# A filter's first layer on GpSimd: products of three inputs in one instruction of 384 columns

## The reference, cut to what matters

```
z = concat([t[:, None], cos(ang), -sin(ang)], axis=-1)     # 256 positions x 33 inputs
h = sin(fr * (z @ w1 + b1))                                # 33 -> 64 hidden
h = sin(fr * (h @ w2 + b2))
h = sin(fr * (h @ w3 + b3))
h = h @ w4                                                 # then decay, convolution by FFT
```

## Time and profile before

| | us |
|---|---|
| median of 3 runs | 2062.11 |
| the profiled execution's own time | 2062.2 |
| its span | 2060.3 |
| TensorE busy (9213 matmuls) | 2010.0 |
| VectorE busy | 1322.0 |
| ScalarE busy | 924.0 |
| GpSimd busy | 384.6 |

### The profile page before, as it was taken

The page is one execution under the profiler, slowest core; times in us unless marked ns, Lnnn a source line. Parts: engine busy times, 40 slices in busy tenths (PEclk is TensorE's granted clock), DMA queues, the critical chain, the costliest instruction groups (busy, mean ns, idle before and its releaser), DMA issues.

```text
span 2060.3 us, 23555 instructions
## 1 busy us (share of the span) xinstructions
PE 2010.0 (98%) x9213; PEld 1595.5 (77%) x9213; DVE 1322.0 (64%) x1684; ACT 924.0 (45%) x1218; POOL 384.6 (19%) x588
## 2 busy tenths in 40 slices
PE   5899999999999999999999999999999999999999
PEld 1268788777878878787888888888888888878887
DVE  4867678798675779878875665644555445444443
ACT  1155534555644544354554444544444444433332
POOL 0000004999999950000000000000000000000000
PEclk9999999999999999999999999999999999999999
DMA  9977667555576675554446555555556655655654
GB/s 344 367 244 252 207 221 243 170 175 167 175 227 190 190 227 183 161 176 148 153 145 204 184 184 185 183 191 191 190 185 193 195 184 188 200 164 187 201 185 162
DMA packets 206242, 407.93 MB, mean 198 GB/s; under 512 B 8826, under 2 KB 15027, under 8 KB 205491
## 3 DMA queue, kind: packets, MB, share of 16 engines
q1 hardware_dynamic: 190480, 376.07, 55.6%
q10 hardware_dynamic: 13892, 23.88, 3.5%
q0 software_dynamic: 1760, 6.49, 1.6%
HBM read 404.31 MB, written 2.10 MB: 197 GB/s over the span
## 4 chain that ended last, share of the span: by engine, by line
PE 72%; POOL 19%; DVE 4%; DMA 3%; issue 2%; ACTq 0%; ACT 0%; SPq 0%; DVEq 0%; POOLq 0%
PE ps L432 44%; PE ps L439 22%; POOL proj L2316 17%; PE pm L520 4%; DMA raw<-in_ada_w 2%; POOL h3T L2316 1%; DVE mod_part L1161 1%; DVE raw_lo L410 1%; PE pm L532 1%; POOL proj L2295 1%; PE ps L520 1%; PE pm L895 0%; PE pm L584 0%; DMA proj<-in_z 0%; DMA rows_b<-in_hgrn_norm_g 0%
## 5 line engine op out<-in xcount | busy, mean ns | idle before, releaser
L410 DVE TENSOR_TENSOR raw_lo<-raw,w_hi 128x1024 fp32r<-128x1024 f32 (+1 forms) x648 | 800.1, 1238 | 565.5 <-ACT w_hi L401 555.8
L401 ACT ACTIVATE w_hi<-raw 128x1024 fp32r<-128x1024 f32 (+1 forms) x648 | 680.3, 1051 | 788.4 <-PE ps L439 761.4
L432 PE MATMUL ps<-w_hi,h_hi 128*128 128x512 f32 (+1 forms) x2336 | 934.6, 401 | 3.7 <-DVE h_lo L977 3.0
L432 PE MATMUL ps<-w_hi,h_lo 128*128 128x512 f32 (+1 forms) x2336 | 908.6, 389 | 0.0
L439 PE MATMUL ps<-raw_lo,h_hi 128*128 128x512 f32 (+1 forms) x2336 | 622.8, 388 | 7.7 <-DVE raw_lo L410 7.6
L432 PEld LDWEIGHTS ps<-w_hi,h_hi 128*128 128x128 f32 x2336 | 441.4, 189 | 103.4 <-issue 9.6
L439 PEld LDWEIGHTS ps<-raw_lo,h_hi 128*128 128x128 f32 x2336 | 436.8, 189 | 102.6 <-DVE raw_lo L410 12.2
L432 PEld LDWEIGHTS ps<-w_hi,h_lo 128*128 128x128 f32 x2336 | 441.6, 189 | 92.9 <-issue 7.4
L2316 POOL TENSOR_TENSOR proj<-proj 128x128 f32<-128x128 f32 x264 | 178.9, 683 | 12.9
L2316 POOL TENSOR_TENSOR proj<-proj,w1T 128x128 f32<-128x128 f32 x165 | 101.8, 625 | 12.3 <-DMA proj<-in_z 5.1
L432 PE MATMUL ps<-w_hi,hid_hi 128*128 128x512 f32 x256 | 100.8, 394 | 0.0
(11 more groups left out here) (322 smaller groups left out, 1146.2 us busy)
## 6 DMA issues: line engine op xcount, KB each, us to landing
raw<-in_w_in SPq DMA_DIRECT2D x136, 1024.0 KB, 5.3
raw<-in_w_ffn_gate SPq DMA_DIRECT2D x44, 1024.0 KB, 5.2
raw<-in_w_ffn_up SPq DMA_DIRECT2D x44, 1024.0 KB, 5.1
raw<-in_w_ffn_down SPq DMA_DIRECT2D x44, 1024.0 KB, 5.1
raw<-in_ada_w SPq DMA_DIRECT2D x32, 1024.0 KB, 7.5
raw<-in_w_out SPq DMA_DIRECT2D x32, 1024.0 KB, 5.2
proj<-in_ada_w ACTq DMA_DIRECT2D x16, 1024.0 KB, 5.2
raw<-in_w_br_hyena SPq DMA_DIRECT2D x8, 1024.0 KB, 5.2
```

The costliest lines, as they stand in the source:

```text
L401: nc.scalar.activation(w_hi[:, p % HRING, :, 0:gm.width(j)], raw[:, k % RING, e:e + HT, 0:gm.width(j)], ACT.Copy).then_inc(hi_done, 1)
L410: nc.vector.tensor_tensor(raw_lo[:, k % RING, e:e + HT, 0:gm.width(j)], raw[:, k % RING, e:e + HT, 0:gm.width(j)], w_hi[:, p % HRING, :, 0 ...
L432: nc.tensor.matmul(ps[pair][:, t, 0:gm.width(j)], l[:, tok], hi[:, i, 0:gm.width(j)], start=(k == 0 and l is x_hi), stop=False)
```

## The change

The products and their errors are made for the three inputs of a group at once: `p_`, `e_` and `q_` become tiles of 3x128 columns, read from `z_k` in one piece, and the weights are broadcast along the 128 positions of each of the three. A group has 9 such instructions of 384 columns. The running sum stays an input at a time, 8 instructions of 128 columns each. It is in a stricter order: where the errors of sum and product were interleaved in 9 stages an input, there are now 7 stages for a group's products and 7 for each of its inputs, 28 a group. A group thus has 33 instructions instead of 51, and all have 363 instead of 561. The three wide tiles and the two narrow ones lie in both halves of `proj`.

```diff
-        f_tmp = proj[:, 0, R_F + 9 * P:R_F + 16 * P].rearrange("p (q n) -> p q n", q=7)
+        f_wide = [proj[:, t, R_F + c * P:R_F + (c + FK) * P].rearrange("p (k n) -> p k n", k=FK) for t, c in ((0, 9), (0, 12), (1, 11))]
+        f_tmp = [proj[:, t, R_F + c * P:R_F + c * P + P] for t, c in ((0, 15), (1, 9))]
...
                 pool.wait_ge(sig(f"z_in{e % 2}"), 32 * (e // 2 + 1))
-                p_, e_, s_, b_, d_, t_, q_ = (f_tmp[:, q] for q in range(7))
+                p_, e_, q_ = f_wide
+                s_, b_ = f_tmp
                 acc = h3T[:]
-                for j in range(FK):
-                    z_, zh, zl = (z_k[e % 2][:, q, j] for q in range(3))
-                    w_, wh, wl = (w1T[:, q, e * FK + j:e * FK + j + 1].to_broadcast([P, P]) for q in range(3))
-                    n = 17 * (FK * e + j)
-                    for stage in (((p_, z_, w_, ALU.mult), (e_, zh, wh, ALU.mult)),
-                                  ((e_, e_, p_, ALU.subtract), (s_, acc, p_, ALU.add), (q_, zl, wh, ALU.mult)),
-                                  ((e_, e_, q_, ALU.add), (b_, s_, acc, ALU.subtract)),
-                                  ((q_, zh, wl, ALU.mult), (d_, s_, b_, ALU.subtract), (t_, p_, b_, ALU.subtract)),
-                                  ((e_, e_, q_, ALU.add), (d_, acc, d_, ALU.subtract)),
-                                  ((q_, zl, wl, ALU.mult), (t_, t_, d_, ALU.add)),
-                                  ((e_, e_, q_, ALU.add),),
-                                  ((t_, t_, e_, ALU.add),),
-                                  ((acc, s_, t_, ALU.add),)):
-                        for o, x, y, op in stage:
-                            g.tensor_tensor(o, x, y, op).then_inc(sig("sum_step"), 1)
-                            n += 1
-                        pool.wait_ge(sig("sum_step"), n)
+                z_, zh, zl = (z_k[e % 2][:, q] for q in range(3))
+                w_, wh, wl = (w1T[:, q, e * FK:e * FK + FK].unsqueeze(2).to_broadcast([P, FK, P]) for q in range(3))
+                n = (9 + 8 * FK) * e
+                products = (((p_, z_, w_, ALU.mult), (e_, zh, wh, ALU.mult)),
+                            ((e_, e_, p_, ALU.subtract), (q_, zl, wh, ALU.mult)),
+                            ((e_, e_, q_, ALU.add),), ((q_, zh, wl, ALU.mult),),
+                            ((e_, e_, q_, ALU.add),), ((q_, zl, wl, ALU.mult),),
+                            ((e_, e_, q_, ALU.add),))
+                sums = [(((s_, acc, p_[:, j], ALU.add),), ((b_, s_, acc, ALU.subtract),),
+                         ((p_[:, j], p_[:, j], b_, ALU.subtract),), ((b_, s_, b_, ALU.subtract),),
+                         ((b_, acc, b_, ALU.subtract), (p_[:, j], p_[:, j], e_[:, j], ALU.add)),
+                         ((p_[:, j], p_[:, j], b_, ALU.add),), ((acc, s_, p_[:, j], ALU.add),)) for j in range(FK)]
+                for stage in itertools.chain(products, *sums):
+                    for o, x, y, op in stage:
+                        g.tensor_tensor(o, x, y, op).then_inc(sig("sum_step"), 1)
+                        n += 1
+                    pool.wait_ge(sig("sum_step"), n)
                 pool.sem_inc(sig("z_used"), 1)
```

More of the change, by code:

```diff
@@ L1 @@
+import itertools
 import math
```

## The result

The changed kernel took 2080.65 us in the median of 6 runs (2072.48 to 2087.72), the kernel before 2060.97 us in the median of its 6 runs (2059.35 to 2063.93). The ratio is 1.0091, 95% interval 1.006 to 1.0123: 0.9% slower. It was forecast at 2074.3 us, between 2060 and 2086 us. Run again on another occasion the same kernel gave 2086.6 us in the median of 4 and 1.0113 (1.0085 to 1.0141). The profiled execution is a long one of the first six, 2086.15 us with a span of 2084.3 us, 24.0 us more than the span before. So the profile has to be explained by 24 us, and the median by 20.

What follows compares the result with a forecast made beforehand. VectorE was taken to bound two stretches, TensorE everything else. 2062.2 us + 4.4 (first stretch) + 7.7 (second) + 1.7 (clock) - 1.7 (won at the last sums) gave 2074.3 us, range 2060 to 2086 us.

Steps and rivals of the forecast that it cites:

- The bound and the sign: VectorE bounds two stretches, about 31 and 80 us, TensorE the rest; 0.6% slower, with slower at 0.73.
- GpSimd's wide sum: A 384-column GpSimd sum takes 1.05 us undisturbed; the last sum ends near 720 us.
- The price of a meeting: Each wide sum that a two-input VectorE instruction meets adds 0.55 us to VectorE's time.
- First tight stretch: 340 to 371 us: eight meetings with group 0's wide sums at 0.55 us, 4.4 us, all reaching TensorE.
- Second tight stretch: About 405 to 487 us: 21 or 22 wide sums, 14 met at 0.55 us, 7.7 us reaching TensorE.
- The clock: Longer waits bring one more drop of TensorE's clock to 1.2 GHz, half in VectorE's shadow: 1.7 us.
- Outside the same delays cost nothing: From 499 us on, VectorE's delays lie in its free 85 us and cost nothing.
- What was won: GpSimd ends earlier, VectorE's 3.96 us wait for the last sum goes, and 1.7 us are gained.
- A: Holding does not grow with instruction width: 2060.5 us, or 2051.5 us faster; chance 0.17 together with B, 0.09 faster.
- B: GpSimd's lateness from 339 to 749 us decides, so faster: at best 2060.5 us; chance 0.17 together with A.
- C: A wide sum costs more than three narrow ones, GpSimd ends late: 2081 us at 1.38 us; within the forecast's 0.74.
- D: 9 and 22 wide sums all met at 0.60 us, 18.6 us, two clock drops: 2085 us; within the forecast's 0.74.

Runs made afterwards that it cites:

- `dma_mid`: Changed kernel with the next group's two input DMAs issued mid-group instead of ahead of its first two wide products: 2076.02 us, ratio 1.0071.
- `wide_single`: Changed kernel with a wait for sum_step behind each GpSimd instruction: 2076.6 us, ratio 1.0072.
- `narrow_order`: Changed kernel with each wide instruction issued as three of 128 columns, same order, tiles and stages: 2061.02 us, ratio 1.0002.
- `pause`: Changed kernel with groups 0 and 2 narrow and GpSimd waiting before group 3 until TensorE is through part 116: 2056.3 us, ratio 0.9975.
- `no_sums`: Changed kernel with all of GpSimd's sums left out, input DMAs kept: 2051.16 us, ratio 0.9957.
- `narrow_single`: Changed kernel with wide instructions issued as three of 128 columns and a wait for sum_step behind each: 2085.14 us, ratio 1.0116.

## Why the prediction was right, and where its sizes were off

The loss was forecast at 12.1 us and is 19.7 us in the median. The median lies inside the forecast range, but not by much: 4 of the 10 executions of the change are above its upper end of 2086 us, and so is the median of the later four. The mechanism held; the terms go in order.

**The bound and the sign: right.** VectorE is the bound in two stretches, and the two engines shut each other out for the length of an instruction. Shown from both sides: the narrow form in the changed order is as fast as before, and a kernel without sums is 0.43% faster.

**GpSimd's wide sum: right.** Forecast 1.05 us. Undisturbed it took 0.82 to 0.85 us as a product with a broadcast weight (two in 1.63 us) and 1.02 us as a sum of two full inputs:

```profile
408.10 1.63 POOL L2319 TENSOR_TENSOR proj<-proj,w1T 128x384 f32<-128x384 f32 x2
409.81 1.02 POOL L2319 TENSOR_TENSOR proj<-proj 128x384 f32<-128x384 f32 x1
```

The last sum came at 686.8 us and not near 720: 31.6 us a group instead of 34. I had taken 1.05 us for all nine, but five of them are the shorter products.

**The price of a meeting: right for one, with a kind left out.** L1360's maximum rose by 0.56 us. L412 behind one wide sum is 2.04 to 2.07 us, forecast 2.1. Not forecast were delays of 1.4 to 2.0 us at the heads of groups, where VectorE comes while GpSimd issues its DMAs and then stays out for both products. There were five in the profile, four of them over 1.8 us, about 5 us in all against single meetings. `dma_mid`, without them, was at 1.0071, the change at 1.0091 and 1.0113 later. That would be 4 to 9 us, but the intervals of 1.0071 and 1.0091 overlap, and `dma_mid` also had 3.2 us less of the wait for L1341.

**First tight stretch: 4.4 us, right in size, by some luck.** VectorE's work took 5.0 us more, and TensorE's was late by 4.3 us more at 405 us. But group 0's nine wide sums brought 3.3 us of it and not 4.4. The rest is the L412 of 3.15 us at the head of group 1. I had placed that group's wide sums near 376 to 390 us, where VectorE is free, but the issue of its DMAs began at 373.56 us, inside the stretch. Its later sums made VectorE busy for 25.34 instead of 21.23 us and cost nothing, as forecast.

**Second tight stretch: the term that was mis-sized.** Forecast 7.7 us, measured 15.45 us of VectorE's time. The step "these 82 us see 2.4 sets of wide sums" failed: the sets began at 408, 439, 472 and 503 us, so six sums of the first, two whole sets and five sums of the fourth fell into it, 29 and not 21 or 22. Groups came each 31.6 us, and the stretch itself became 15 us longer by what it suffered: lateness there brings in more wide sums. At the prediction's own two thirds and 0.55 us, 29 sums are an estimated 10.6 us. Three long delays at heads of groups add 3.2 us over single meetings. The last 1.6 us is not placed; the forecast counted two-input instructions alone, and COPY and TENSOR_SCALAR, with one input, were held too.

**The clock: 1.7 us, about 1 us by the traces.** From 341 to 521 us it was low for some 14 us instead of 7, and for 7 instead of 3.4 near 636 us, so there were more drops than forecast, and half of the added time would be 5 us. But TensorE lost little by them: it became 16.3 us later in the second stretch, 0.9 us more than VectorE's 15.45 us, and near 636 us most of the added low time is the wait itself.

**"Outside the same delays cost nothing": this step failed in one place.** TensorE never waited for L412 from 521 to 769 us. But its one wait for L1341 grew from 1.9 to 5.6 us, and the work was another 3.8 us late there. The wait goes with the eight L1337 ahead of it: 7.0 us of them and 5.5 to 5.6 us of wait in both profiles of the change, 4.3 and 2.4 us in `dma_mid` and `wide_single`, 4.2 and 2.3 us with wide sums in groups 5 to 10 alone, 3.8 and 1.9 us before, 2.2 and 0.3 us without sums. In the change a group's wide sums fell just on them. The 85 us that VectorE has free from 499 us on did not help, since TensorE waits for the end of this work.

**What was won: 1.7 us, right.** Matmul by matmul, TensorE was 25.0 us late before the sine and 23.0 us behind it.

Of the rivals, A (holding by pieces) fell with the first L412 over 1.53 us. B (GpSimd's lateness is what matters) fell as well: GpSimd was 63 us earlier and the kernel later. C did not come about. D came nearest to the profiled execution, with 2085 us against 2086.15. Its 18.6 us of meetings are near what VectorE lost in the two stretches, 20.4 us, but by other counts: 29 wide sums in the second and not 22, and less than 0.60 us for most. Its two full drops of the clock did not cost 6 us.

The Trainium skill, page "SBUF — State Buffer", section "Who interferes with whom", calls what VectorE and GpSimd share an exclusive lock, which whoever issues first has for the whole instruction. The 384-column sums agree: up to 0.84 us of delay for a product of 0.82 to 0.85 us.

## What to carry to other kernels

Look for the stretches in which the second engine is the bound before making a helper's instructions longer: GpSimd got 15% faster in its own work and the kernel 0.9% slower, because each wide sum shuts VectorE out for up to 0.84 us instead of 0.30. Wide instructions belong where VectorE has room, and a semaphore that counts TensorE's parts is enough to put them there (here 0.25% faster than the kernel before). Where another engine waits for the end of a piece of VectorE's work, it has no room, whatever its busy share over the stretch. Two engines that disturb each other are best measured by leaving one out: GpSimd's sums cost the kernel before 9 us, and of that only VectorE's 3.96 us at their end stood in a view as a wait for GpSimd. The rest is in the durations of VectorE's instructions.

## What was not expected of the hardware

- GpSimd's issue of two DMAs (1.29 us) and the two ready products behind it (1.62 us) kept a VectorE instruction of 1.225 us for 3.15 us. Of 128-column products five or six in a row did much the same (1.7 us of delay in `narrow_order`, 2.2 us in `pause`). With the DMAs elsewhere, the same pair delayed VectorE by 0.84 us at most.
- A 384-column GpSimd product with a broadcast operand takes 0.82 to 0.85 us against 1.02 us for a sum or difference of two full ones; at 128 columns it was 0.38 against 0.46 us. No run tells whether the operand or the operation makes it.
- VectorE's COPY and TENSOR_SCALAR, with one SBUF input, were held by wide sums too: 1.01 us for a COPY of 0.23 us. MAX8 was not: 281 to 430 ns, and 287 to 431 ns in `no_sums`.
- TensorE stood for 22.4 us, and its granted clock was 0.50 in the whole stretch of 24 us that spans the wait (`narrow_single`).
